# Second expert table: 64 of 256 tokens by gathered rows and VectorE passes, the other 192 in five TensorE passes for six

## The chip, the core and the metric

The kernel runs as one program on one core of one Trainium2 chip. The metric is the device time of one execution in microseconds (us), the median of several runs. The engines named below are TensorE (PE, its weight loads PEld), VectorE (DVE), ScalarE (ACT), GpSimd (POOL) and SyncE (SP), which here only issues DMAs.

## What is computed

One block on 256 tokens of width 2048: RMSNorm, an input projection, a state-space group and a windowed attention group, an output projection, and then the part that the change is about, a product-key retrieval of experts:

```python
def peer_ffn(xn, wq, keys, u_tab, v_tab):        # 16384 experts, 8 heads, top 16 of each
    q = (xf @ wq).reshape(t, PEER_HEADS, 2, PEER_HALF)
    sc = jnp.einsum("thpk,hpnk->thpn", q, keys)
    ...                                           # top 16 of both halves, top 16 of their sums
    gate = jax.nn.softmax(top, axis=-1)           # eidx, gate: 128 experts for each token
    u = jnp.take(u_tab, ib, axis=0)
    act = jax.nn.gelu(jnp.einsum("thkd,td->thk", u, xb), approximate=False)
    v = jnp.take(v_tab, ib, axis=0)
    return jnp.einsum("thk,thkd->td", gb * act, v)
...
h = h + peer_ffn(rmsnorm(h, norm2_g[i]), peer_wq[i], peer_keys[i], peer_u[i], peer_v[i])
return rmsnorm(h, norm_f_g)
```

All in float32. Each token uses 128 (head, expert) pairs of 16384 experts.

## The kernel before

Both expert tables are streamed whole, in 128 chunks of 128 experts (1 MB each), in two pieces of 512 KB. A ring of four pieces (`raw`, `high`, `low`) carries every streamed matrix of the kernel, and one chain serves it. SP loads a piece into `raw` (L325) when VectorE has finished the piece four before it in the ring (`lo_done`); ScalarE rounds it into `high` (L442), once TensorE has finished the piece four before it (`used`); VectorE forms the rest, `raw` minus `high`, in `low` (L686); TensorE multiplies. To reach float32 accuracy each product is three passes: high by high, high by low, low by high.

- **First table** (`product`, L1253 to L1255): for each chunk 48 matmuls of 256 columns give scores of 128 experts by 256 tokens; ScalarE takes them through Gelu into `big` (`expert_step`, L452). Meanwhile VectorE does the routing between its cuts (`route`, `center`, `share`), and GpSimd scatters the gates of the picked experts by 256 indirect DMAs with add (L430) into `gate_scratch`, a dense array of 128 chunks by 128 experts by 256 tokens in HBM, which SP cleared earlier.
- **Second table**: for each chunk VectorE multiplies Gelu and gates (`weights`, L1195), ScalarE rounds that (`round_w`, L653), VectorE forms the low part (L1198), and TensorE adds weights by table rows into all eight PSUM banks: 2 halves x 2 token blocks x 3 passes x 2 banks, 24 matmuls of 512 columns (`row_products`, L1476 to L1480). SP loads chunk after chunk, and behind the two pieces of each the gates of a chunk (`gate_load`, L377) after a wait on `w_ok`. VectorE's order in a chunk is: cut, gates, cut, low part of the weights.
- **End**: TensorE adds the residual from `h_back` (L1506); then for each block of 128 tokens follow square (L670), root (L674), VectorE's product (L1221) and the store (L409).

Of the kernel before, what the change touches and what calls it, by code (L numbers as in the profile page):

```python
# [20 lines left out]
ds = bass.ds  # L21
# [15 lines left out]

# [20 lines left out]
RING = 4  # L58

# [37 lines left out]
def build(nc, x_t, small, id_iota, w_in, w_out, w_q, keys, u_tab, v_tab, g_f, out):  # L97
    h_scratch = nc.dram_tensor("h_scratch", (P, KT * T), F32).ap()
    cs_scratch = nc.dram_tensor("cs_scratch", (1, SSD_HEADS * BLK), F32).ap()
    gate_scratch = nc.dram_tensor("gate_scratch", (N_KEYS, P, T), F32).ap()  # L100
    gate_cells = gate_scratch.rearrange("r c (t o) -> (r c t) o", o=1)

    with ExitStack() as ctx:
# [30 lines left out]
        w_lo = sb(ctx, "w_lo", 2 * T, F32R)
# [45 lines left out]
        SCORES = QZ  # L180
# [17 lines left out]
        assert ROUTE >= (ROUTE_CHUNKS + 8) * T and PICKS + 768 <= SCORES  # L198
# [3 lines left out]
        h_sum = view(XBC + 10 * T, T)  # L202
        rstd1 = view(TOK_T + 4 * SSD_HEADS, T)
# [82 lines left out]
        scattered = [sem(f"scattered{r}") for r in range(ROUTE_STEPS)]  # L286
        gate_back = [sem(f"gate_back{k}") for k in range(2)]
# [30 lines left out]
        def _(sp):  # L318
# [44 lines left out]
            def clear(group):  # L363

                dst = gate_scratch[ds(ZERO_CHUNKS * group, ZERO_CHUNKS)].rearrange("r c t -> c r t")
                src = zeros.rearrange("p (o t) -> p o t", o=1).broadcast_to([P, ZERO_CHUNKS, T])
                sp.dma_start(dst, src).then_inc(cleared, 16)
# [5 lines left out]
            sp.dma_start(h_scratch, h_sb).then_inc(h_saved, 16)  # L373
            load_all(u_tab, C_U, N_KEYS)
# [4 lines left out]
            for j in range(2):  # L379
                load(C_V_TAB + j, (C_V_TAB + j) % 2, v_tab[j])  # L380
            for r in range(ROUTE_STEPS):
                sp.wait_ge(scattered[r], 16 * TOPK)
# [13 lines left out]
            for q in range(H_PARTS + 2):  # L396
                second_table(q, q + 1)
                if q < H_PARTS:
                    n = KT * T // H_PARTS
# [5 lines left out]
            for tb in range(TB):  # L405
                for q in range(2):
                    sp.wait_ge(last_ok, 2 * tb + q + 1)
                    n = D // 2
                    sp.dma_start(out[tb * P:(tb + 1) * P, q * n:(q + 1) * n],  # L409
                                 big[:, (2 * tb + q) * n:(2 * tb + q + 1) * n]).then_inc(stored, 16)  # L410
            sp.wait_ge(stored, 16 * 2 * TB)
# [3 lines left out]
        def _(pool):  # L415
# [8 lines left out]
            for r in range(ROUTE_STEPS):  # L424
                h, tb = r // TB, r % TB
                pool.wait_ge(picks_ok, r // BATCH_STEPS + 1)
                if h:
                    pool.wait_ge(scattered[(h - 1) * TB + tb], 16 * TOPK)
                for at in range(r * TOPK, (r + 1) * TOPK):
                    nc.gpsimd.indirect_dma_start(  # L430
                        out=gate_cells, out_offset=bass.IndirectOffsetOnAxis(ap=cells_sb[:, at:at + 1], axis=0),
                        in_=gates_sb[:, at:at + 1], in_offset=None, compute_op=ALU.add).then_inc(scattered[r], 16)
# [3 lines left out]
        def _(act):  # L436
# [178 lines left out]
            with act.Fori(0, KT // 2 - 1) as i:  # L615
# [7 lines left out]
            def expert_step(c, par):  # L623
                cut_high(c + 1, 1 - par)
                at = (c - C_U) * T
                take(c, par, big[:, ds(at, T)], ACT.Gelu)

            def expert_pairs(lo, hi):
                with act.Fori(lo // 2, hi // 2) as i:
                    for j in range(2):  # L630
                        expert_step(C_U + 2 * i + j, (C_U + j) % 2)
# [6 lines left out]
            expert_pairs(0, 2)  # L638
            act.wait_ge(h_saved, 16)
            done = 2  # L640
            for b in range(ROUTE_BATCHES):
                expert_pairs(done, BATCH_CHUNKS * (b + 1) + 2)
                done = BATCH_CHUNKS * (b + 1) + 2
                soften(b)
            expert_pairs(done, ROUTE_CHUNKS + 8)
            act.wait_ge(picks_ok, ROUTE_BATCHES)
            expert_pairs(ROUTE_CHUNKS + 8, N_KEYS - 2)

            def round_w(e, par):
# [3 lines left out]
                nc.scalar.activation(w_hi[:, par * T:(par + 1) * T], w_full[par], ACT.Copy).then_inc(wh_ok, 1)  # L653

            expert_step(C_V_TAB - 2, C_V_TAB % 2)
            expert_step(C_V_TAB - 1, (C_V_TAB + 1) % 2)
            round_w(0, C_V_TAB % 2)
            with act.Fori(0, N_KEYS // 2 - 1) as i:
                for j in range(2):
                    e = 1 + 2 * i + j  # L660
                    par = (C_V_TAB + 1 + j) % 2
                    cut_high(C_V_TAB + e, par)
                    round_w(e, par)
            cut_high(C_END - 1, (C_END - 1) % 2)
            round_w(N_KEYS - 1, (C_END - 1) % 2)

            for tb in range(TB):
                act.wait_ge(sum_ok, tb + 1)
                acc = ps[:, 4 * tb:4 * tb + 4, :]
# [919 lines left out]
```

## Time and profile before

| what | value |
|---|---|
| median of 3 runs | 1900.62 us (1900.42 to 1902.73) |
| the profiled execution: its time / its span | 1903.04 us / 1901.2 us |
| granted TensorE clock, mean | 0.994 |
| busy share of the span: PE, DVE, ACT, POOL | 98%, 61%, 47%, 23% |
| second table, PE | about 1189 to 1892 us |

A row of the views has the engine's line, what it writes and reads, its count, the busy time and the mean of one, and then the time the engine sat idle before it and who ended that. The idle time of an engine that does not set the pace costs nothing. A busy TensorE is not one at its peak, since the ends of pipelined matmuls are modelled; the distance from start to start of equal steps is what a step costs.

### The profile page before, as it was taken

How to read it: one execution, taken by the hardware profiler on the slowest of the kernel's cores; microseconds unless marked ns; L12 is line 12 of the kernel's file. 1: busy time of each engine (PE TensorE's matmuls, PEld its weight loads, DVE VectorE, ACT ScalarE, POOL GpSimd, SP SyncE). 2: the span in 40 equal slices, each digit the busy share in tenths (PEclk: the TensorE clock that was granted, in tenths of full speed). 3: DMA queues.
4: the chain of work that ended last, by engine and by line, in shares of the span. 5: the costliest groups of instructions: out<-in, count | busy, mean ns of one | idle time of the engine just before them, and what ended most of it. 6: DMA issues, size and time to landing. Idle time of an engine off the chain costs nothing.

```text
span 1901.2 us, 36770 instructions
## 1 busy us (share of the span) xinstructions
PE 1861.1 (98%) x12735; PEld 1727.7 (91%) x12735; DVE 1153.9 (61%) x2075; ACT 899.3 (47%) x1212; POOL 431.4 (23%) x262
## 2 busy tenths in 40 slices
PE   7999979999999999999999999999999999999998
PEld 7998879999999999999999999888888888888886
DVE  7786676667888885344434434555555555555554
ACT  6545734434366666443344334444444444444443
POOL 0000000000028787877777710000000000000000
PEclk9999989999999999999999999999999999999999
DMA  7643548886557777777777765876666666666663
GB/s 246 216 174 134 166 134 271 276 254 225 181 176 183 183 183 177 191 183 178 184 185 183 177 184 175 279 240 217 217 217 219 217 213 220 215 218 216 220 215 117
DMA packets 167158, 383.03 MB, mean 201 GB/s; under 512 B 50240, under 2 KB 83152, under 8 KB 166736
## 3 DMA queue, kind: packets, MB, share of 16 engines
q1 hardware_dynamic: 130080, 379.25, 60.3%
q0 software_dynamic: 37040, 3.32, 5.7%
q8 instruction: 19, 0.31, 0.1%
q14 instruction: 19, 0.16, 0.0%
HBM read 361.37 MB, written 21.13 MB: 201 GB/s over the span
## 4 chain that ended last, share of the span: by engine, by line
PE 93%; DVE 2%; issue 2%; ACT 2%; DVEq 0%; DMA 0%; ACTq 0%; SPq 0%
PE ps L1253 18%; PE ps L1254 18%; PE ps L1255 18%; PE ps L1476 12%; PE ps L1480 12%; PE ps L1478 12%; ACT high L442 1%; PE ps L1506 0%; PE ps L1447 0%; DVE big L1012 0%; DVE big L1003 0%; DVE big L696 0%; DVE big L1014 0%; DVE big L984 0%; PE ps L1350 0%
## 5 line engine op out<-in xcount | busy, mean ns | idle before, releaser
L686 DVE TENSOR_TENSOR low<-raw,high 128x1024 fp32r<-128x1024 f32 x638 | 770.3, 1224 | 633.4 <-ACT high L442 586.0
L1253 PE MATMUL ps<-act_hi,high 128*128 128x256 f32 x3056 | 872.9, 286 | 24.3 <-DVE act_lo L719 13.1
L1254 PE MATMUL ps<-act_lo,high 128*128 128x256 f32 x3056 | 867.7, 284 | 0.0
L1255 PE MATMUL ps<-act_hi,low 128*128 128x256 f32 x3056 | 867.6, 284 | 0.0
L442 ACT ACTIVATE high<-raw 128x1024 fp32r<-128x1024 f32 x638 | 657.0, 1054 | 432.6 <-PE ps L1480 378.8
L1253 PEld LDWEIGHTS ps<-act_hi,high 128*128 128x128 f32 x3056 | 589.6, 193 | 29.0 <-issue 16.5
L1254 PEld LDWEIGHTS ps<-act_lo,high 128*128 128x128 f32 x3056 | 589.7, 193 | 0.1
L1255 PEld LDWEIGHTS ps<-act_hi,low 128*128 128x128 f32 x3056 | 589.6, 193 | 0.0
L430 POOL DMA_INDIRECT gate_scratch<-gates_sb,cells_sb x256 | 429.9, 1679 | 591.9 <-DVE gates_sb L1167 470.5
L1476 PE MATMUL ps<-high,w_hi 128*128 128x512 f32 x1024 | 315.5, 389 | 1.3 <-ACT big L452 1.3
L1480 PE MATMUL ps<-high,w_lo 128*128 128x512 f32 x1024 | 315.2, 389 | 0.0
L1478 PE MATMUL ps<-low,w_hi 128*128 128x512 f32 x1024 | 315.2, 389 | 0.0
L1476 PEld LDWEIGHTS ps<-high,w_hi 128*128 128x128 f32 x1024 | 192.0, 188 | 41.2 <-ACT big L452 1.5
L1480 PEld LDWEIGHTS ps<-high,w_lo 128*128 128x128 f32 x1024 | 192.2, 188 | 39.9
L1478 PEld LDWEIGHTS ps<-low,w_hi 128*128 128x128 f32 x1024 | 192.2, 188 | 39.9
L452 ACT ACTIVATE big<-ps 128x256 f32 (+1 forms) x128 | 49.3, 385 | 338.1 <-PE ps L1255 335.4
L591 ACT ACTIVATE act_hi<-big (+1 forms) x32 | 13.4, 418 | 95.0 <-DVE big L1014 52.6
L1198 DVE TENSOR_TENSOR w_lo<-side,w_hi 128x256 fp32r<-128x256 f32 x128 | 53.4, 418 | 2.4 <-ACT w_hi L653 2.4
L1195 DVE TENSOR_TENSOR side<-big,side 128x256 f32<-128x256 f32 x128 | 53.4, 418 | 0.0
L653 ACT ACTIVATE w_hi<-side 128x256 fp32r<-128x256 f32 x128 | 51.1, 399 | 0.8 <-DVE side L1195 0.8
L735 DVE TENSOR_TENSOR big<-ps,big 128x256 f32<-128x256 f32 (+2 forms) x47 | 19.7, 421 | 45.9 <-PE ps L1255 45.8
L452 ACT ACT_TABLE_LOAD x22 | 28.2, 1283 | 35.0 <-PE ps L1255 31.3
(158 smaller groups left out, 571.0 us busy)
## 6 DMA issues: line engine op xcount, KB each, us to landing
raw<-u_tab SPq DMA_DIRECT2D x256, 512.0 KB
raw<-v_tab SPq DMA_DIRECT2D x256, 512.0 KB
raw<-w_in SPq DMA_DIRECT2D x62, 512.0 KB
raw<-w_out SPq DMA_DIRECT2D x32, 512.0 KB
gate_scratch<-side SPq DMA_DIRECT2D x32, 512.0 KB, 6.8
raw<-w_q SPq DMA_DIRECT2D x32, 512.0 KB
side<-gate_scratch SPq DMA_DIRECT2D x128, 128.0 KB, 3.4
gate_scratch<-gates_sb,cells_sb POOLq DMA_INDIRECT x256
```

The source lines that it names most:

```text
L430: nc.gpsimd.indirect_dma_start(out=gate_cells, out_offset=bass.IndirectOffsetOnAxis(ap=cells_sb[:, at:at + 1], axis=0), in_=gates_sb[:, at ...
L442: nc.scalar.activation(slot(high, s), slot(raw, s), ACT.Copy).then_inc(hi_done, 1)
L452: nc.scalar.activation(dst, ps[:, par, 0:T], func).then_inc(taken, 1)
L686: V.tensor_tensor(slot(low, s), slot(raw, s), slot(high, s).bitcast(F32), ALU.subtract).then_inc(lo_done, 1)
L1195: V.tensor_tensor(w_full[par], gelu, gate_in[par], ALU.mult).then_inc(w_ok, 1)
L1198: V.tensor_tensor(w_lo[:, par * T:(par + 1) * T], w_full[par], w_hi[:, par * T:(par + 1) * T].bitcast(F32), ALU.subtract).then_inc(wl_ok, 1)
L1253: mm(acc, wh, a_hi, start=(kk == 0), stop=False)
L1254: mm(acc, wh, a_lo, start=False, stop=False)
L1255: ins = mm(acc, wl, a_hi, start=False, stop=(kk == KT - 1))
L1476: mm(acc[n], wh, vh[n], start=start, stop=False, skip_group_check=True)
L1478: mm(acc[n], wh, vl[n], start=False, stop=False, skip_group_check=True)
L1480: ins = mm(acc[n], wl, vh[n], start=False, stop=stop, skip_group_check=True)
```

## The change

Tokens 192 to 255 leave the second table's matmuls (`SPARSE` = 64, `DENSE` = 192). The first table is unchanged on TensorE, but ScalarE takes its result in two steps, 192 columns to `big` and 64 to `act_out`, and SP writes the latter to `act_scratch` in HBM, once every four chunks (32 DMAs). Gates are scattered densely for 192 tokens only: GpSimd issues 192 scatters and 8 small copies where it issued 256 scatters. The 64 x 128 picks of the other tokens are laid over 128 partitions, 64 in each (64 "units"). For each unit GpSimd gathers 128 rows of `v_tab`, of 8 KB each (1 MB), into one of three buffers; VectorE adds them, times gate times Gelu, to `acc_s` (128 x 2048). The Gelu values come by 64 gathers of one number for each partition. Before that, `acc_s` gets the residual of the 64 tokens by 16 transposes on TensorE and a copy on ScalarE, in the query stage. The unit stands behind the weights of a chunk, in 64 of the chunks 10 to 120. In the last chunks the two halves of `acc_s` are added and normalized.

For the dense 192 tokens the weights lie as [high of 64 tokens, high of 128, high of the 64 again, low of 64, low of 128]. One pass with 128 weight columns does high and low of the 64 tokens at once, a second their high by the table's low; the 128 tokens keep three passes. The part that came from the low weights lies in the partitions 64 to 127 of four banks, and is added at the end by four more matmuls.

```diff
+SPARSE = 64
+DENSE = T - SPARSE
+SLOTS_HALF = 8
+UNITS = SLOTS_HALF * PEER_HEADS
+ROWS = 3
+EXPORT = 4
+FIRST_UNIT, LAST_UNIT = 9, 121
...
@@ SP
-            load_all(u_tab, C_U, N_KEYS)
+            def save_act(g):
+                dst = act_scratch[EXPORT * g:EXPORT * (g + 1)].rearrange("r c t -> c r t")
+                sp.wait_ge(taken, C_U + EXPORT * (g + 1))
+                sp.dma_start(dst, act_out[g % 2].rearrange("p (r t) -> p r t", t=SPARSE)).then_inc(act_saved, 16)
...
             sp.wait_ge(used, 2 * C_V_TAB)
+            save_act(N_KEYS // EXPORT - 1)
@@ GpSimd, behind the scatters
+            def gather_row(n):
+                h, k = n // SLOTS_HALF, SLOTS_HALF + n % SLOTS_HALF
+                if n >= ROWS:
+                    pool.wait_ge(row_used, n - ROWS + 1)
+                nc.gpsimd.indirect_dma_start(
+                    out=row_in[n % ROWS], out_offset=None, in_=v_rows,
+                    in_offset=bass.IndirectOffsetOnAxis(ap=half_ix[:, h, 0, k:k + 1], axis=0)).then_inc(rows_in[n % ROWS], 16)
...
+            pool.wait_ge(act_saved, 16 * (N_KEYS // EXPORT))
+            for n in range(per):
+                gather_cell(n)
+            for n in range(UNITS):
+                for m in range(per + 4 * n, min(per + 4 * n + 4, UNITS)):
+                    gather_cell(m)
+                if n + ROWS < UNITS:
+                    gather_row(n + ROWS)
@@ ScalarE
-                take(c, par, big[:, ds(at, T)], ACT.Gelu)
+                nc.scalar.activation(view(e * DENSE, DENSE), ps[:, par, 0:DENSE], ACT.Gelu)
...
+                nc.scalar.activation(act_out[e // EXPORT % 2][:, at:at + SPARSE], ps[:, par, DENSE:T],
+                                     ACT.Gelu).then_inc(taken, 1)
...
-                nc.scalar.activation(w_hi[:, par * T:(par + 1) * T], w_full[par], ACT.Copy).then_inc(wh_ok, 1)
+                nc.scalar.activation(w_t[par][:, W_HI], w_full[:, :], ACT.Copy)
+                nc.scalar.activation(w_t[par][:, W_HI2], w_full[:, B_TOK], ACT.Copy).then_inc(wh_ok, 1)
@@ VectorE
+            def sparse_unit(n):
...
+                if n:
+                    dve.wait_ge(row_used, n)
+                else:
+                    dve.wait_ge(h_tok_ok, 1)
+                dve.wait_ge(rows_in[n % ROWS], 16 * (n // ROWS + 1))
+                V.scalar_tensor_tensor(out=acc_s, in0=row_in[n % ROWS], scalar=share_sb[:, n:n + 1], in1=acc_s,
+                                       op0=ALU.mult, op1=ALU.add).then_inc(row_used, 1)
...
+                cut_low_piece(C_V_TAB + e, par, 0)
+                weights(e, par, lambda: cut_low_piece(C_V_TAB + e, par, 1))
+                if unit < UNITS and (e - FIRST_UNIT + 1) * UNITS >= (unit + 1) * span:
+                    sparse_unit(unit)
+                    unit += 1
@@ TensorE
+            def narrow_rows(par, hf, start=False, stop=False):
...
+                for n in range(2):
+                    mm(acc[n], w[:, DENSE:DENSE + 2 * SPARSE], vh[n], start=start, stop=False, skip_group_check=True)
+                for n in range(2):
+                    ins = mm(acc[n][0:SPARSE], w[:, B_TOK], vl[n], start=False, stop=stop, skip_group_check=True)
...
-                    for tb in range(TB):
-                        ins = row_products(par, hf, tb, start=start)
-                    ins.then_inc(used, 1)
+                    narrow_rows(par, hf, start=start)
+                    wide_rows(par, hf, start=start).then_inc(used, 1)
...
+            pe.wait_ge(low_out, 1)
+            for n in range(4):
+                ins = mm(ps[0:SPARSE, 4 + n, :], ident[SPARSE:, SPARSE:], low_sb[SPARSE:, n * 512:(n + 1) * 512],
+                         start=False, stop=True, skip_group_check=True)
```

TensorE, the loop over the second table before: one half of a chunk (`high`, `low` are the table's parts, `w_hi`, `w_lo` the weights'; x2 is two banks).

```order
L1476 MATMUL ps<-high,w_hi 128x512 x2
L1478 MATMUL ps<-low,w_hi 128x512 x2
L1480 MATMUL ps<-high,w_lo 128x512 x2
L1476 MATMUL ps<-high,w_hi 128x512 x2
L1478 MATMUL ps<-low,w_hi 128x512 x2
L1480 MATMUL ps<-high,w_lo 128x512 x2
```

The same half of a chunk in the changed kernel (`w_even` holds all parts of the weights of an even chunk).

```order
L1665 MATMUL ps<-high,w_even 128x512 x2
L1667 MATMUL ps<-low,w_even 64x512 x2
L1677 MATMUL ps<-high,w_even 128x512 x2
L1679 MATMUL ps<-low,w_even 128x512 x2
L1681 MATMUL ps<-high,w_even 128x512 x2
```

Twelve matmuls are ten, and nothing else stands between them.

VectorE, the last chunk of the second table before (the loop's body has the same four operations):

```order
L686 TENSOR_TENSOR low<-raw,high 128x1024
L1195 TENSOR_TENSOR side<-big,side 128x256
L686 TENSOR_TENSOR low<-raw,high 128x1024
L1198 TENSOR_TENSOR w_lo<-side,w_hi 128x256
L1216 TENSOR_SCALAR big<-big 128x1
```

VectorE in the middle of the second table of the changed kernel, two chunks that follow each other, with a unit behind each:

```order
L821 TENSOR_TENSOR low<-raw,high 128x1024
L1366 TENSOR_TENSOR w_full<-big,side 128x192
L821 TENSOR_TENSOR low<-raw,high 128x1024
L1369 TENSOR_TENSOR w_odd<-w_full,w_odd 128x192
L1357 SCALAR_TENSOR_TENSOR big<-big,share_sb 128x2048
L821 TENSOR_TENSOR low<-raw,high 128x1024
L1366 TENSOR_TENSOR w_full<-big,side 128x192
L821 TENSOR_TENSOR low<-raw,high 128x1024
L1369 TENSOR_TENSOR w_even<-w_full,w_even 128x192
L1357 SCALAR_TENSOR_TENSOR big<-big,share_sb 128x2048
```

A unit (`L1357`) now stands between a chunk's weights and the next chunk's first cut, in 4 of 7 chunks, and the two operations on weights are a quarter narrower.

## Rows read from the trace of the kernel before

**Rows 1.** The page: busy us of each engine (share of the span); the chain's shares.

```profile
PE 1861.1 (98%) x12735; PEld 1727.7 (91%) x12735; DVE 1153.9 (61%) x2075; ACT 899.3 (47%) x1212; POOL 431.4 (23%) x262
...
PE 93%; DVE 2%; issue 2%; ACT 2%; DVEq 0%; DMA 0%; ACTq 0%; SPq 0%
```

**Rows 2.** Busy us (instructions) of each engine, PEclk, DMA share, GB/s by stretches.

```profile
1110.00:1180.00 70.00, 70.00 (x586) 70.00 (x585) 29.04 (x25) 27.91 (x36) 0.00 (x0) 1.00 0.54 181
1300.00:1400.00 100.00, 100.00 (x443) 82.79 (x442) 57.09 (x75) 44.77 (x55) 0.00 (x0) 1.00 0.65 215
600.00:700.00 100.00, 99.95 (x831) 99.55 (x830) 88.67 (x305) 66.21 (x74) 77.38 (x46) 1.00 0.73 182
```

**Rows 3.** Groups by line, second table, 1300 to 1800 us.

```profile
L686 DVE TENSOR_TENSOR low<-raw,high 128x1024 fp32r<-128x1024 f32 x185 | 226.8, 1226 | 214.5 <-ACT high L442 214.5
L1476 PE MATMUL ps<-high,w_hi 128*128 128x512 f32 x736 | 226.5, 389 | 0.0
...
L442 ACT ACTIVATE high<-raw 128x1024 fp32r<-128x1024 f32 x184 | 195.2, 1061 | 277.1 <-PE ps L1480 277.1
...
L1198 DVE TENSOR_TENSOR w_lo<-side,w_hi 128x256 fp32r<-128x256 f32 x92 | 38.4, 418 | 0.0
...
L653 ACT ACTIVATE w_hi<-side 128x256 fp32r<-128x256 f32 x92 | 36.7, 399 | 0.0
```

**Rows 4.** VectorE in order of time, second table: start, us, operation, idle before it.

```profile
1190.16 0.42 DVE L1195 TENSOR_TENSOR side<-big,side 128x256 f32<-128x256 f32 x1
1190.50 1.22 DVE L686 TENSOR_TENSOR low<-raw,high 128x1024 fp32r<-128x1024 f32 x1
...
1200.90 1.23 DVE L686 TENSOR_TENSOR low<-raw,high 128x1024 fp32r<-128x1024 f32 x1 [1.16 <-ACT high L442]
1202.04 0.42 DVE L1198 TENSOR_TENSOR w_lo<-side,w_hi 128x256 fp32r<-128x256 f32 x1
...
1207.48 0.42 DVE L1198 TENSOR_TENSOR w_lo<-side,w_hi 128x256 fp32r<-128x256 f32 x1
```

**Rows 5.** The DMA view, 1300 to 1800 us.

```profile
DMA packets 39699, 108.37 MB, mean 217 GB/s; under 512 B 4414, under 2 KB 16190, under 8 KB 39699
...
side<-gate_scratch SPq DMA_DIRECT2D x92, 128.0 KB, 3.2
```

**Rows 6.** The DMA view, 8 to 16 us, reads in rows of 4 KB.

```profile
DMA packets 1152, 3.27 MB, mean 409 GB/s; under 512 B 256, under 2 KB 384, under 8 KB 1152
...
q1 hardware_dynamic: 1152, 3.27, 103.2%
```

**Rows 7.** Stretches as in rows 2, around the start of the second table.

```profile
1188.00:1196.00 8.00, 7.40 (x33) 6.13 (x34) 5.56 (x8) 4.78 (x7) 0.00 (x0) 1.00 0.93 290
1189.00:1190.00 1.00, 1.00 (x6) 0.82 (x5) 0.98 (x1) 0.94 (x1) 0.00 (x0) 1.00 0.98 213
```

**Rows 8.** DMA issues: KB each, median us to landing.

```profile
h_back<-h_scratch SPq DMA_DIRECT2D x4, 512.0 KB, 6.5
...
g_last<-g_f SPq DMA_DIRECT2D x2, 512.0 KB, 5.5
```

**Rows 9.** Groups by line, whole span, the nearest kin of what is added.

```profile
L1263 PE MATMUL ps<-big,side 128*128 128x256 f32 x42 | 11.3, 430 | 2.5 <-ACT big L556 2.5
...
L1506 PE MATMUL ps<-consts,h_back 128*128 128x128 f32 x64 | 7.5, 275 | 0.0
...
L984 DVE SCALAR_TENSOR_TENSOR big<-big,side 128x256 f32<-128x256 f32 x16 | 6.7, 478 | 0.1
...
L1221 DVE SCALAR_TENSOR_TENSOR big<-ps,big,g_last 128x1024 f32<-128x1024 f32 x4 | 5.0, 1280 | 0.1
```

**Rows 10.** The chain in order of time, its end: start, us, what.

```profile
1879.77 3.57 PE ps L1506 x32
...
1892.41 1.98 ACT big L670 x2
1895.62 1.28 DVE big L1221
```

More of the change, by code:

```diff
@@ L202, in build @@
         h_sum = view(XBC + 10 * T, T)
+        GELUS = N_KEYS * DENSE
+        row_in = [view(GELUS + k * D, D) for k in range(ROWS)]
+        low_sb = view(GELUS, D)
+        acc_s = view(GELUS + ROWS * D, D)
+        assert GELUS + ROWS * D >= SCORES + TB * 2 * PEER_HEADS * N_KEYS and GELUS + (ROWS + 1) * D <= N_KEYS * T
         rstd1 = view(TOK_T + 4 * SSD_HEADS, T)
@@ L286, in build @@
         scattered = [sem(f"scattered{r}") for r in range(ROUTE_STEPS)]
+        swapped = sem("swapped")
+        act_saved = sem("act_saved")
+        cell_ok = sem("cell_ok")
+        cell_in = [sem(f"cell_in{b}") for b in range(ROUTE_BATCHES)]
+        rows_in = [sem(f"rows_in{k}") for k in range(ROWS)]
+        row_used = sem("row_used")
+        h_turned = sem("h_turned")
+        h_tok_ok = sem("h_tok_ok")
+        half_moved = sem("half_moved")
+        s_summed = sem("s_summed")
+        s_squared = sem("s_squared")
+        s_var = sem("s_var")
+        s_root = sem("s_root")
+        s_done = sem("s_done")
+        s_stored = sem("s_stored")
+        low_sum = sem("low_sum")
+        low_out = sem("low_out")
         gate_back = [sem(f"gate_back{k}") for k in range(2)]
@@ new lines, in _ @@
+            for b in range(ROUTE_BATCHES):
+                pool.wait_ge(picks_ok, b + 1)
+                hs = slice(2 * b, 2 * b + 2)
+                nc.gpsimd.dma_start(half_v[0:SPARSE, hs, :, SLOTS_HALF:], swap_v[SPARSE:, hs, :, 0:SLOTS_HALF]).then_inc(swapped, 16)
+                nc.gpsimd.dma_start(half_v[SPARSE:, hs, :, 0:SLOTS_HALF], swap_v[0:SPARSE, hs, :, SLOTS_HALF:]).then_inc(swapped, 16)
+                scatter(2 * b, 0)
+                pool.wait_ge(swapped, 32 * (b + 1))
+                scatter(2 * b, 1)
+                scatter(2 * b + 1, 0)
+                scatter(2 * b + 1, 1)
@@ L435, in _ @@
+            nc.gpsimd.dma_start(row_in[1][0:SPARSE], acc_s[SPARSE:]).then_inc(half_moved, 16)
+            pool.wait_ge(s_done, 1)
+            nc.gpsimd.dma_start(out[DENSE:], acc_s[0:SPARSE]).then_inc(s_stored, 16)
         @block.scalar
@@ L1030, in _ @@
             inverse_root(3, rs_v[:, 0:T], rs_r[:, 0:T], [(7, T, 0, D)])
+            own.step(V.memset(acc_s[SPARSE:], 0.0))
             def score_take(m, j):
@@ L1166, in share @@
                 own.settle()
-                V.tensor_tensor(by_head(gates_sb[:, cols]), part, wide(r_total), ALU.mult).then_inc(picks_ok, 1)
+                part = by_block(pick[2])
+                per_head = r_total.rearrange("p (h b o) -> p b h o", b=TB, o=1)
+                own.step(V.tensor_tensor(first(gates_sb), part[:, 0], per_head[:, 0].broadcast_to([P, 2, TOPK]), ALU.mult))
+                for dst in (half_v, swap_v):
+                    ins = V.tensor_tensor(dst[:, hs, 1, :], part[:, 1], per_head[:, 1].broadcast_to([P, 2, TOPK]), ALU.mult)
+                ins.then_inc(picks_ok, 1)
             own.step(V.tensor_tensor(r_diag, ident, iota, ALU.mult))
@@ L1204, in v_step @@
+            unit = 0
+            half_s = slice(0, SPARSE)
+            for e in range(1, N_KEYS):
+                par = (C_V_TAB + e) % 2
                 cut_low_piece(C_V_TAB + e, par, 0)
                 weights(e, par, lambda: cut_low_piece(C_V_TAB + e, par, 1))
-            with dve.Fori(0, N_KEYS // 2 - 1) as i:
-                for j in range(2):
-                    v_step(1 + 2 * i + j, (C_V_TAB + 1 + j) % 2)
-            v_step(N_KEYS - 1, (C_END - 1) % 2)
-            dve.wait_ge(gf_in, 16 * 2)
```

294 lines of the change are left out of this document (197 added, 97 removed).

## Prediction

> **What bounds the kernel now.** Read the page first: TensorE is busy in 98% of the span and is 93% of the chain that ended last [rows 1]. Then the stretches, since each stage has its own limit: in both tables TensorE is busy 100% at the full granted clock (1.00, its level of 2.4 GHz), VectorE 41% and 57%, ScalarE 40% and 45% [rows 2]. Then the groups of the second table with their idle times: ScalarE's rounding sat idle 277.1 of 500 us, and what ended that was a matmul; VectorE's cut sat idle 214.5 us until the rounding [rows 3]. So ScalarE waits for TensorE, VectorE for ScalarE, and TensorE for nobody. A step costs its distance from start to start: the low part of the weights starts at 1202.04 and again at 1207.48, so a chunk takes 5.44 us, and each of its 24 matmuls 5.44/24 = 0.2267 us [rows 4] (389 ns, the mean in rows 3, is one matmul with its pipeline).
>
> The question is what comes next when TensorE needs less. Two resources get work for what TensorE gives up: VectorE, and the 16 DMA engines.
>
> **TensorE.** Four matmuls fewer in each of 128 chunks: 512 x 0.2267 = 116.1 us less. The passes with 64 weight columns still stream 512 columns, so they count in full. A chunk is then 20 x 0.2267 = 4.53 us.
> Added on TensorE: 16 transposes with float32 operands in the query stage. The nearest step is the residual's, 16 of which (32 instructions) take 3.57 us [rows 10]: +3.6 us, on the path, since TensorE has no idle time in the stages around it.
> Added at the end: the residual matmuls stay 32 in number, and four matmuls of 512 float32 columns fold the low part. One of 256 such columns is two instructions of about 0.22 us from start to start (11.3 us for 42 gives 0.27 as upper bound) [rows 9], so one of 512 columns is about 0.9 us: 3.6 us in front of the last sum. Behind that the end is the old one, 1892.4 to 1901.2 [rows 10]. The two blocks' squares and products still fit one behind the other: the wide block's sum is ready about 3.4 us ahead of the last one, VectorE's two products of one block take 2 x 1.28 us [rows 9]. So +3.6 us.
>
> **VectorE, by chunk.** From start to start a cut takes 1202.04 - 1200.90 = 1.14 us and an operation on 256 columns of weights 1190.50 - 1190.16 = 0.34 us [rows 4]; on 192 columns I take 0.28. A unit is one operation over 2048 columns, which no row shows. Between 256 columns at 478 ns and 1024 at 1280 ns a column costs 1.04 ns [rows 9], so 2048 take 1280 + 1024 x 1.04 = 2350 ns. With a unit in 4 of 7 chunks: 2 x 1.14 + 2 x 0.28 + 2.35 x 4/7 = 4.18 us against TensorE's 4.53: 92%, not the bound, but it was 54%.
> A unit may hold up the chain even so. Put TensorE's end of chunk e-2 at 0. ScalarE rounds the second piece of chunk e until 1.3 and the weights until 1.8, VectorE is through at about 2.7, and TensorE wants chunk e at 4.53. A unit from 2.7 to 5.0 delays the next chunk's first cut, whose rounding was done at 3.5; that chunk is through at 7.8, wanted at 9.06. If a second unit stands there, the third chunk is through at 12.9, wanted at 13.6, and then comes a chunk without one. The margin stays above 0.7 us, so I cost the units at nothing while the loads come in time. Without that margin each of 64 units costs 2 x 1.14 + 0.56 + 2.35 - 4.53 = 0.66 us, 42 us in all.
>
> **ScalarE** rounds two pieces (1061 ns each) and the weights in two steps, at most 2 x 399 ns [rows 3]: 2.9 of 4.53 us. In the first table it takes the scores in two steps, at most 0.4 us more of a chunk in which it is idle for over half [rows 2]. The split and the save to `act_scratch` lie ahead of the first weights and of the load of chunk 2 on SP: +1.0 us (0 to 4), for about 0.4 us stand on TensorE's path. **GpSimd** and the additional operations of `share` lie beside a TensorE that is 99.95% busy where VectorE is busy 88.67 of 100 us [rows 2]; 64 fewer scatters more than pay for the 8 copies. The 32 saves run in pieces of 256 B where the DMA share is 0.54 to 0.73 [rows 2]; the ring has 2 chunks, 11 us, to hide them: 0 (up to 5). The longer straight-line code I cost at nothing (0 to 3).
>
> **DMA, by chunk.** In steady state a chunk brings 1.049 MB of table and 0.131 MB of gates at 217 GB/s [rows 5], share 0.65 [rows 2]. New: 1.049 + 0.098 (gates of 192 tokens) + 4/7 x 1.049 (a unit's 128 rows of 8 KB) = 1.746 MB in 4.53 us, that is 385 GB/s. That is 1.8 times today's rate, and the dearest new resource. What can 16 engines do? Three readings bound it:
> - a full queue of 4 KB rows moved 409 GB/s for 8 us, with a third of the packets small [rows 6]: 1.746/0.409 = 4.27 us, under TensorE's 4.53;
> - today's share as if it were linear: 217/0.65 = 334 GB/s: 5.23 us;
> - the stretch at the start of the second table, where gates, `h_back` and table are asked for together: 290 GB/s at share 0.93 [rows 7], as linear 312 GB/s: 5.60 us.
> I build the value from packets. In rows 6, 8 us x 16 engines x 1.032 = 132 engine-us went to 768 packets of 4 KB and 384 small ones: 0.155 us for 4 KB. Rows of 1 KB move 213 GB/s at share 0.98 [rows 7], so about 0.075 us each. A chunk then needs (256 + 4/7 x 256) x 0.155 + 128 x 0.07 + about 1 for the completions = 72.4 engine-us, over 16 engines 4.53 us: just TensorE's own pace. Two streams whose requests wait on consumers will not keep every engine full; I take 95%, 4.77 us. Gathers run from chunk 10 to about 116, some 107 chunks: 107 x (4.77 - 4.53) = +25.7 us.
> A rule of the Trainium skill speaks against even that much. "DMA: Bandwidth & Descriptors", section Specifications, gives about 358 GB/s as the limit of HBM for a core. The 409 GB/s of rows 6 are above it for 8 us, so this trace does not agree. By it a chunk takes 4.88 us and the term is +37 us, not +26.
>
> **The sum**, against the profiled execution's own 1903.0 us: 1903.0 - 116.1 + 3.6 + 3.6 + 1.0 + 25.7 = 1820.8. The median of the runs is 2.4 us lower, 1900.6: so 1818.4, say 1819 us.
>
> **The rivals.**
> (a) TensorE sets the pace all through, DMA and units stay hidden: 1795.1 - 2.4 = 1793 us. For it: 409 GB/s, and three row buffers that hold 5 chunks' worth of gathers. Against it: it needs 385 GB/s over 500 us of two streams, which no row shows.
> (b) The DMA engines have one flat ceiling midway between the readings of 409 and 312 GB/s, 360: 1.746/0.360 = 4.85 us, 107 x 0.32 = +34: 1827 us, between 1822 and 1845 (340 GB/s). For it: of rows 2 and 7 no stretch shows over 290. Against it: rows 6. The limit of the skill's page named above, 358 GB/s, is this case with a cause of its own, and gives 1830.
> (c) The linear reading is right, 334 GB/s: 107 x (5.23 - 4.53) = +75: 1868 us. For it: rows 5 and 7 give 312 to 334 by themselves. Against: rows 6 shows packets overlapping at a share over 1, so a share below 1 overstates what a packet needs.
> (d) VectorE's units find no margin because each load is late: +42 us over (a), 1835 us.
> (e) Slower than before: the gathers crowd out SP's loads. A piece is loaded only after the cut of the piece four before it, so two chunks take at least one load's landing L, the rounding 1.06, the cut 1.14, some 0.7 for signals and 0.7 for a unit in the way: a chunk takes (L + 3.6)/2. Today a load of 128 KB behind a piece lands in 3.2 us [rows 5], pieces behind others in 5.5 to 6.5 us [rows 8]. At L = 5.5 the chunk is 4.55, still hidden; at L = 6.5 it is 5.05, +56 us. The saving of 107.9 us is used up when 107 chunks take 5.54 us each, at L = 7.5; at L = 8 a chunk takes 5.8 and the time is 1929 us. For it: up to 3 MB of gathers can stand in GpSimd's queue at once, beside 1 MB of SP's. Against it: VectorE needs a unit only every 7.9 us, so if engines share evenly a gather is in flight for 5.2 of 7.9 us, SP has 200 GB/s in that time and 400 in the rest, 268 on the mean against the 253 that it needs.
> The skill's page named above has in its section "Queues, rings and completion order" that an engine takes its queues in turn by packets; if a gather's packets are the larger ones, SP gets less than half. No row shows both queues under load.
> That the change does nothing can be left out: the matmuls are gone from TensorE's order.
>
> **How the numbers follow.** Forecast (chunks at 4.65 to 4.80 us, 1806 to 1822): 0.42. (a) 0.17, (b) 0.13, (c) 0.14, (d) 0.04, (e) 0.10. The likeliest gives 1819. The range leaves out (e) and the upper part of (c), to 1880, and reaches down to (a) less its small terms, 1792. A measurement can tell 0.2%, some 4 us. Faster: all but (e), 0.90; within 0.2%, a point inside (e), 0.01; slower 0.09.
>
> **What would show it.** TensorE's start-to-start of matmuls stays 0.227 us; chunks 0 to 9 and 117 to 127 take 4.53 us each. In the middle a chunk takes 4.77, and the chain of waits there runs TensorE from VectorE's cut, that from ScalarE, that from a load of `v_tab`. The DMA view shows about 366 GB/s and a share near 1.0. Under (a) ScalarE still waits for TensorE and the rate is 385; under (b) and (c) the rate is flat at 360 or 334 in every slice; under (d) VectorE has no idle time; under (e) the rate falls below 315 while raw pieces take over 7.5 us to land. The prediction is wrong if TensorE's stretch in the first table grows, or if VectorE waits on `rows_in`: I have three buffers hide each gather, 16 us ahead.

## The result and the profile after

The changed kernel takes 1835.9 us (median of 4 runs, 1833.4 to 1842.1) against 1901.4 of the kernel before: a ratio of 0.966, 95% interval 0.963 to 0.969. That is 65 us less; the forecast was 82 less, and the range held the time. The profiled execution took 1842.05 us, span 1840.3, and was the slowest of the four, so what is read from its trace lies some 6 us above the median.

The page of the changed kernel: busy times, the DMA share and GB/s by fortieths of the span, and the chain's shares.

```profile
PE 1771.6 (96%) x12247; PEld 1605.1 (87%) x12247; DVE 1282.2 (70%) x2166; ACT 874.5 (48%) x1434; POOL 521.6 (28%) x336
...
DMA  7554538776557778777777555599999999999994
GB/s 252 204 189 138 175 91 252 229 244 217 191 188 189 188 189 189 189 188 189 189 188 257 188 188 188 196 307 334 358 342 348 359 359 351 338 363 348 347 322 127
...
PE 67%; DMA 15%; DVE 8%; issue 5%; ACT 4%; SPq 0%; DVEq 0%; ACTq 0%
```

TensorE is still busy in 96% of the span, but its share of the chain fell from 93% [rows 1] to 67%, and DMA stands in it with 15%. From the 27th of the 40 slices to the last but one, the second table, the DMA share is 9 tenths and more.

Busy time of PE, PEld, DVE, ACT and POOL (with counts), granted clock, DMA share and GB/s, in the late first table and in the middle of the second:

```profile
1000.00:1100.00 100.00, 100.00 (x836) 100.00 (x835) 41.51 (x36) 39.77 (x68) 0.00 (x0) 1.00 0.59 186
1250.00:1750.00 500.00, 474.61 (x2000) 354.94 (x1999) 422.94 (x461) 259.61 (x402) 145.01 (x95) 0.99 0.95 350
```

The first table is as it was [rows 2]. In the second, TensorE is idle for 25 of 500 us, and the engines move 350 GB/s where they moved 215. VectorE is busy 85%, was 57%.

The groups of VectorE and ScalarE there, and the waits (engine, line, waited for: us, times, longest):

```profile
L821 DVE TENSOR_TENSOR low<-raw,high 128x1024 fp32r<-128x1024 f32 x200 | 244.3, 1222 | 54.4 <-ACT high L553 52.9
L553 ACT ACTIVATE high<-raw 128x1024 fp32r<-128x1024 f32 x202 | 214.0, 1060 | 182.0 <-DMA raw<-v_tab 144.2 <-PE ps L1681 36.1
L1357 DVE SCALAR_TENSOR_TENSOR big<-big,share_sb 128x2048 f32<-128x2048 f32 x58 | 136.0, 2346 | 0.1
...
L1366 DVE TENSOR_TENSOR w_full<-big,side 128x192 f32<-128x192 f32 x100 | 35.3, 353 | 23.8 <-DMA side<-gate_scratch 23.6
```

```profile
ACT high L553 <- DMA raw<-v_tab: 144.2, 118, 4.2
DVE low L821 <- ACT high L553: 52.9, 77, 3.3
PEld ps L1665 <- DVE low L821: 38.7, 31, 3.5
ACT high L553 <- PE ps L1681: 36.1, 40, 2.7
...
DVE w_full L1366 <- DMA side<-gate_scratch: 23.6, 17, 2.3
```

The reader is to compare this with [rows 3]. There ScalarE's rounding waited 277 us for TensorE. Here it waits 144 us for a load of `v_tab`, 118 times of 202, and 36 us for TensorE. The chain is turned round: ScalarE waits for DMA, VectorE for ScalarE, TensorE for VectorE.

The DMA view of the same stretch (KB each, median us to landing):

```profile
DMA packets 52757, 174.79 MB, mean 350 GB/s; under 512 B 7005, under 2 KB 19817, under 8 KB 45438
...
raw<-v_tab SPq DMA_DIRECT2D x200, 512.0 KB, 6.3
side<-gate_scratch SPq DMA_DIRECT2D x100, 96.0 KB, 6.4
big<-v_tab,half_sb POOLq DMA_INDIRECT x57, 9.1
```

A piece now lands 6.3 us after it was asked for, and the gates after 6.4 where the kernel before had 3.2 [rows 5]; for the pieces of the second table before no landing is on record. A unit's gather takes 9.1 us and is in time: VectorE has no wait for `rows_in`. The median for the pieces rests on 50 of the 200 loads, those whose landing the trace has, and they differ widely:

```profile
DMA to landing us min/median/max: 3.1/6.3/8.7
```

How long a chunk takes is read from TensorE, from the first matmul of a chunk (L1665) to the first of the next: 4.60 us where it waits for nobody, as in the chunks 118 to 125, without gathers; 4.99 us on the mean of the 107 chunks from 10 on (5.00 below). It is not an even pace. Of the 107 chunks 71 take under 4.75 us; 21 take more than 5.2, up to 7.8, and hold 34 of the 42 us that the 107 take beyond 4.60 each.

Three small terms. TensorE in order of time, in a stretch where it waits for nobody, two matmuls in each row:

```profile
1217.10 0.63 PE L1667 MATMUL ps<-low,w_even 128*64 128x512 f32 x2
...
1219.40 0.63 PE L1667 MATMUL ps<-low,w_even 128*64 128x512 f32 x2
```

From one half of a chunk to the next 2.30 us pass for ten matmuls, 0.230 us each; before it was 0.2267. The 16 transposes of the residual and the four last matmuls, by line:

```profile
L1718 PE MATMUL ps<-big,consts 64*64 64x512 f32 x8 | 3.6, 595 | 0.0
...
L1638 PE MATMUL ps<-consts,big 128*64 128x128 f32 x16 | 1.9, 272 | 0.0
```

And the end of the chain:

```profile
1815.61 3.64 PE ps L1705 x32
...
1827.67 1.98 ACT big L805 x2
```

The end lasts from 1815.6 to 1840.3, 24.7 us; before, 1879.8 to 1901.2 [rows 10], 21.4. The four matmuls of L1718 run behind the sum of the 128 tokens, from 1827.6 to 1831.2, and the square of the 64 tokens starts at 1831.24.

### The profile page after: what moved, and what is told of

It reads as the page before. It is cut to its first block, busy times and chain, and to the rows that moved or that the text cites. A ratio compares the mean times of both kernels' runs of the same rounds, so it can differ in the third digit from the quotient of the medians.

```text
span 1840.3 us, 34226 instructions
## 1 busy us (share of the span) xinstructions
PE 1771.6 (96%) x12247; PEld 1605.1 (87%) x12247; DVE 1282.2 (70%) x2166; ACT 874.5 (48%) x1434; POOL 521.6 (28%) x336
## 4 chain that ended last, share of the span: by engine, by line
PE 67%; DMA 15%; DVE 8%; issue 5%; ACT 4%; SPq 0%; DVEq 0%; ACTq 0%
PE ps L1435 19%; PE ps L1436 18%; PE ps L1437 18%; DMA raw<-v_tab 12%; DVE low L821 4%; DMA side<-gate_scratch 4%; ACT high L553 3%; PE ps L1665 2%; PE ps L1679 2%; PE ps L1681 2%; PE ps L1667 2%; PE ps L1677 2%; DVE big L1357 1%; DVE w_full L1366 0%; DVE big L831 0%
## 5 line engine op out<-in xcount | busy, mean ns | idle before, releaser
L497 POOL DMA_INDIRECT gate_scratch<-gates_sb,cells_sb x128 | 213.2, 1666 | 66.2 <-issue 66.2
L517 POOL DMA_INDIRECT big<-v_tab,half_sb x64 | 99.7, 1558 | 362.5 <-DVE big L1357 358.8
L525 POOL DMA_INDIRECT share_sb<-act_scratch,cell_ix x64 | 92.7, 1448 | 239.2 <-DMA act_scratch<-side 220.0
L1357 DVE SCALAR_TENSOR_TENSOR big<-big,share_sb 128x2048 f32<-128x2048 f32 x64 | 150.1, 2346 | 0.1
L497 POOL DMA_INDIRECT gate_scratch<-half_sb x64 | 108.1, 1689 | 19.5 <-issue 19.5
L1665 PE MATMUL ps<-high,w_even 128*128 128x512 f32 x256 | 81.7, 401 | 15.7 <-DVE w_even L1369 14.1
L1665 PE MATMUL ps<-high,w_odd 128*128 128x512 f32 x256 | 81.7, 401 | 12.4 <-DVE w_odd L1369 12.2
L1667 PE MATMUL ps<-low,w_odd 128*64 128x512 f32 x256 | 80.9, 397 | 0.0
L1679 PE MATMUL ps<-low,w_even 128*128 128x512 f32 x256 | 80.7, 396 | 0.0
L1681 PE MATMUL ps<-high,w_odd 128*128 128x512 f32 x256 | 80.5, 396 | 0.0
L1679 PE MATMUL ps<-low,w_odd 128*128 128x512 f32 x256 | 80.5, 396 | 0.0
```

Of the source, the lines that this page charges most:

```text
L497: nc.gpsimd.indirect_dma_start(out=gate_cells, out_offset=bass.IndirectOffsetOnAxis(ap=ix, axis=0), in_=v, in_offset=None, compute_op=ALU. ...
L517: nc.gpsimd.indirect_dma_start(out=row_in[n % ROWS], out_offset=None, in_=v_rows, in_offset=bass.IndirectOffsetOnAxis(ap=half_ix[:, h, 0, ...
L1357: V.scalar_tensor_tensor(out=acc_s, in0=row_in[n % ROWS], scalar=share_sb[:, n:n + 1], in1=acc_s, op0=ALU.mult, op1=ALU.add).then_inc(row_ ...
L1665: mm(acc[n], w[:, DENSE:DENSE + 2 * SPARSE], vh[n], start=start, stop=False, skip_group_check=True)
L1667: ins = mm(acc[n][0:SPARSE], w[:, B_TOK], vl[n], start=False, stop=stop, skip_group_check=True)
L1679: mm(acc[n], wh, vl[n], start=False, stop=False, skip_group_check=True)
```

## The experiments

The question was what holds a chunk at 5.00 us where TensorE needs 4.60. Three answers: the DMA engines are full (ceiling); VectorE has no margin with the units; or the ring is too short for the time that a load now takes (loop). The time is that of one run, or the median of several where a ratio is given. e1 to e5 leave out or spoil a part of the result: their times show what a piece of work costs. The mean of a chunk is read as above, from chunk 10 to chunk 117. In rows of stretches the columns are those of [rows 2].

### e1: units without gathers

```diff
 def gather_row(n):
+    if n < ROWS:                      # only the first three
         nc.gpsimd.indirect_dma_start(...)
...
-    dve.wait_ge(rows_in[n % ROWS], 16 * (n // ROWS + 1))
+    dve.wait_ge(rows_in[n % ROWS], 16)
```

> The gathers of rows are left out after the first three; VectorE's 64 units of 2048 columns stay and use old rows, so the 64 tokens' sums are not computed. Measured so far: a chunk takes 5.00 us in the middle of the second table, and TensorE's own pace there is 4.60. Theory DMA (the 16 DMA engines are full): chunks go to 4.60 us everywhere, time 1836 - 43 = 1793 us. Theory VectorE (the units leave no margin): chunks stay near 5.0, time 1830 to 1836.

1800.1 us. The middle of the second table:

```profile
1250.00:1750.00 500.00, 500.00 (x2176) 384.94 (x2175) 454.02 (x499) 278.39 (x436) 55.39 (x39) 1.00 0.76 250
```

TensorE is without a gap and a chunk takes 4.60 us, with VectorE busy 454 of 500 us. So the units alone hold nothing back where loads come in time; the loss comes with the gathers. From the low part of the first chunk's weights to that of the last it is 624.8 - 582.6 = 42 us between the two profiled executions, and 36 us between this run and the changed kernel's median.

### e2: gathers of half the bytes

```diff
-    out=row_in[n % ROWS], out_offset=None, in_=v_rows,
+    out=row_in[n % ROWS][:, 0:PIECE], out_offset=None, in_=v_halves,   # rows of 4 KB
```

> Each gather after the first three brings rows of 4 KB instead of 8 KB, as many of them; the units stay whole, so half of each sum uses old data. Theory DMA by bytes (350 GB/s): 1.446 MB / 0.350 = 4.13 us, below TensorE's pace, so 4.60 us and 1793 us. Theory DMA by requests (a row costs the same whatever its size): 5.0 and 1836. Theory VectorE: 1836.

1806.7 us, chunks of 4.66:

```profile
1250.00:1750.00 500.00, 497.09 (x2147) 378.55 (x2146) 451.54 (x495) 277.43 (x429) 157.43 (x98) 1.00 0.90 309
```

Near TensorE's pace. The bytes of a row count, the number of requests does not hold the kernel at 5.00; but at 309 GB/s and a share of 0.90 a small loss is left already, which a ceiling of 350 doesn't explain.

### e3: all gathers, units of 64 columns

```diff
-    V.scalar_tensor_tensor(out=acc_s, in0=row_in[n % ROWS], ..., in1=acc_s, ...)
+    V.scalar_tensor_tensor(out=acc_s[:, 0:64], in0=row_in[n % ROWS][:, 0:64], ..., in1=acc_s[:, 0:64], ...)
```

> All gathers stay; a unit on VectorE works on 64 columns instead of 2048, so most of the 64 tokens' sums are left out. Theory DMA: a chunk stays at 4.95 to 5.0 us at 350 GB/s, time 1828 to 1836. Theory VectorE: 4.60 and 1793.

1830.3 us, chunks of 4.85:

```profile
1250.00:1750.00 500.00, 482.15 (x2061) 364.78 (x2060) 317.78 (x474) 266.40 (x413) 115.81 (x97) 0.99 0.98 360
```

VectorE is busy 318 instead of 423 of 500 us, and the time is 6 us less, which one run against a spread of 9 us hardly shows. VectorE as the bound is ruled out, also with loads that come late. But the same bytes went at 360 GB/s, not at 350. That is a first sign against a fixed ceiling, though a weak one: the profiled execution of the changed kernel was its slowest.

### e4: plain copies in place of gathers

```diff
-    nc.gpsimd.indirect_dma_start(out=row_in[n % ROWS], ..., in_=v_rows, in_offset=...)
+    nc.gpsimd.dma_start(row_in[n % ROWS], v_tab[(37 * n) % N_KEYS])
```

> In place of a gather of picked rows GpSimd copies one whole chunk of the table, the same 1 MB in the same 128 rows of 8 KB but contiguous and not indirect; the sums use wrong rows. Theory DMA by bytes: no change, 1830 to 1840. Theory that scattered rows or indirect descriptors are the cost: chunks of 4.6 to 4.8 us, 1793 to 1815.

1827.0 us, chunks of 4.86, 360 GB/s in 1250 to 1750 us. 9 us less than the median, 6 less than the fastest run of the changed kernel. That the rows are scattered and the descriptors indirect costs at most some 9 of the 36 us; how much of the 9 is the spread, one run does not say.

### e5: no loads of gates

```diff
-    sp.wait_ge(w_ok, 2 * i + j + 1)
-    gate_load(2 * i + j + 2, par)
```

> The gates of chunks 2 to 127 are not loaded (old gates are used, so the sums are wrong); all else stays. It takes 128 rows of 768 B from each chunk: 5.6% of the bytes but a quarter of the packets. Theory that the DMA engines are limited by bytes (350 GB/s): 1.648/0.350 = 4.71 us for a chunk, time 1836 - 31 = 1805 us. Theory that each packet has a price (0.07 us or more for a small one): 76.8 - 9 = 67.8 engine-us, 4.4 us, so TensorE's pace of 4.60, 1795 us. Theory that the load's landing behind the gathers sets the pace whatever the share: 4.9 and 1828.

1829.4 us, chunks of 4.87:

```profile
1250.00:1750.00 500.00, 483.38 (x2052) 362.44 (x2051) 429.58 (x472) 261.44 (x410) 150.83 (x97) 0.99 0.93 338
```

The first two forecasts fail: with 26% of the packets gone (39235 of 52757 are left in 500 us) the time should have fallen by 30 us or more by either reading of a full engine. It fell by 6, and the DMA share fell to 0.93. Engines that are the bound don't get idle when work is taken from them. The third forecast fits, 4.9 us and 1828: the landing of a load sets the pace, whatever the share. The edit also takes out SP's wait for `w_ok`, but in the changed kernel SP waited for VectorE's cuts alone (304.5 us of 500).

### e6: the 64-column pass with 128 weight columns

```diff
-    ins = mm(acc[n][0:SPARSE], w[:, B_TOK], vl[n], ...)
+    ins = mm(acc[n], w[:, 0:P], vl[n], ...)
```

> The pass over the table's low part for the 64 tokens gets 128 weight columns instead of 64 (what it adds in the partitions 64 to 127 is wrong). A pair of matmuls is 0.460 us from start to start in the changed kernel and was 0.4533. If the switch between 64 and 128 weight columns costs that: 0.4533 again, about 6 us off the light chunks and little in the full ones, 1830 to 1835. If not, no change: 1834 to 1840.

1836.8 us, but TensorE's rows, two matmuls each, read:

```profile
1214.67 0.62 PE L1667 MATMUL ps<-low,w_odd 128*128 128x512 f32 x2
...
1216.93 0.62 PE L1667 MATMUL ps<-low,w_odd 128*128 128x512 f32 x2
```

2.26 us for ten matmuls, 2.30 before. The 64-column pass among 128-column passes costs 0.03 to 0.04 us in each half of a chunk. In chunks that wait for loads it is not seen.

### e7: the gates of four chunks in one load

```diff
-    gate_scratch = nc.dram_tensor("gate_scratch", (N_KEYS, P, DENSE), F32).ap()
+    gate_scratch = nc.dram_tensor("gate_scratch", (N_KEYS // 4, P, 4 * DENSE), F32).ap()
+    v_quads = v_tab.rearrange("(m a) c d -> m (a c) d", a=4).rearrange("m (c s) d -> m c s d", s=4)
...
+    for e in range(2, N_KEYS):        # written out
+        load(C_V_TAB + e, (C_V_TAB + e) % 2, v_quads[e // 4, :, e % 4, :])
+        if e % 4 == 2 and e // 4 + 1 < N_KEYS // 4:
+            sp.wait_ge(w_ok, e - 1)
+            gate_load(e // 4 + 1)     # 128 rows of 3 KB
```

> Chunks are laid out as expert = 512 m + 4 c + s, so that the gates of four chunks lie side by side for each partition, and come in one load of rows of 3 KB, one group ahead; the stores of the Gelu values and the clearing of the gates get rows four times as long as well. All 256 tokens are computed as in the reference. Same bytes, 96 packets fewer of 446 in a chunk. Theory packets: 128 x 0.07 turn into 32 x about 0.13 engine-us, 5 engine-us or 0.3 us less of a chunk: 4.7 us, 1836 - 32 = 1804 us. Theory bytes: 5.0 and 1830 to 1836, less the 24 us in which VectorE waits for gates at most.

1823.2 us (6 runs, 1814.5 to 1825.3), ratio 0.9595 (0.958 to 0.961). The gain is 13 us, where the count of packets gave 32, and bytes 0 to 6 and up to 24 more for the waits for gates: that doesn't decide between them. The run changed three things at once, the layout, the loading in fours and SP's loop, which e9 and e12 take apart in part.

### e8: a ring of six pieces

```diff
+    raw_more = sb(ctx, "raw_more", 2 * PIECE)      # where act_hi, act_lo were
...
+    for half in range(2):
+        n = 2 * e + half
+        if n >= 6:
+            sp.wait_ge(lo_done, 2 * C_V_TAB + n - 5)   # six pieces back, not four
+        sp.dma_start(raw_slot(n), ...)
```

> The changed kernel with six pieces of raw for the second table instead of four (the two new ones lie where the first table's activations were); bytes, packets, gathers and units are the same, and a load may be asked for two pieces earlier. Theory ceiling (the 16 DMA engines are full at 350 GB/s): 1830 to 1836, chunks of 4.95 to 5.0 us. Theory loop (a piece is asked for only after the cut four pieces before it, and lands 6.3 us later beside the gathers: (6.3 + 3.6)/2 = 4.95 us for a chunk): with six pieces (6.3 + 3.6)/3 = 3.3 us, no limit; then chunks of 4.6 to 4.75 us as far as the engines can (at most about 375 GB/s), 1800 to 1812.

1799.8 us (4 runs, 1799.5 to 1802.0), ratio 0.947 (0.945 to 0.949). Stretch, landing times, waits:

```profile
1250.00:1750.00 500.00, 500.00 (x2176) 385.36 (x2175) 455.12 (x500) 278.82 (x435) 170.66 (x98) 1.00 1.00 376
```

```profile
raw<-v_tab SPq DMA_DIRECT2D x144, 512.0 KB, 7.7
raw_more<-v_tab SPq DMA_DIRECT2D x73, 512.0 KB, 7.8
```

```profile
ACT high L560 <- PE ps L1693: 165.3, 153, 1.5
...
ACT high L560 <- DMA raw<-v_tab: 3.9, 2, 2.0
...
ACT high L560 <- DMA raw_more<-v_tab: 1.2, 2, 0.6
```

All gathers, all units, the same bytes, and TensorE has no gap: chunks of 4.60 us, and the time of e1, where all but three gathers of rows were left out. The engines move 376 GB/s. A piece lands later than before, after 7.7 us instead of 6.3, and hardly anybody waits for it: 5.1 us in all, where it was 144. So 350 GB/s was not a ceiling. It was, but for the loops that e12 takes out of the account, the result of how early the ring let SP ask.

### e9: the layout of e7, gates one chunk at a time

```diff
+    v_chunk = lambda e: v_quads[e // 4, :, e % 4, :]
-    sp.dma_start(gate_in[par], gate_scratch[e])
+    sp.dma_start(gate_in[par], gate_scratch[e // 4, :, g:g + DENSE])   # 128 rows of 768 B as before
```

> The layout of e7 (expert = 512 m + 4 c + s, table rows of a piece 32 KB apart instead of 8, longer rows in the first table's stores), but the gates of each chunk come by themselves, in 128 rows of 768 B one chunk ahead, as in the changed kernel. If the loading of gates in fours was what brought e7 its 12 us: 1832 to 1838. If it was the layout: 1820 to 1826.

1818.3 us (4 runs, 1811.6 to 1822.6), ratio 0.956 (0.953 to 0.959). No slower than e7, so the loading in fours brought nothing; what is left is the layout and SP's written-out loop. Chunks take 4.74 us here and 4.73 in e7.

### e12: the control, loops written out

```diff
-    with sp.Fori(first, end) as i:
-        for j in range(2):
-            load(C_V_TAB + 2 + 2 * i + j, par, v_tab[2 * i + j + 2])
+    for e in range(2, N_KEYS):
+        load(C_V_TAB + e, (C_V_TAB + e) % 2, v_tab[e])
...
-    with act.Fori(0, N_KEYS // 2 - 3) as i:
+    for e in range(1, N_KEYS - 5):
```

> The changed kernel with the second table's loops on SP and ScalarE written out, as e8 to e11 have them (e7 and e9 on SP alone), and with the ring of four pieces and the plain layout: the control for those runs. If the written-out loops were part of their gain, e.g. because SP asks for a piece sooner: 1815 to 1828. If the two more pieces (e8) and the layout (e7, e9) did it: 1832 to 1840, chunks of 4.95 to 5.0 us at 350 GB/s.

1829.2 us (4 runs, 1824.0 to 1830.8), ratio 0.961 (0.959 to 0.962):

```profile
1250.00:1750.00 500.00, 483.54 (x2059) 361.16 (x2058) 432.66 (x473) 263.52 (x409) 148.29 (x99) 1.00 0.98 361
```

Just above the first forecast, below the second: of the 36 us that e8 gains, some 7 are the written-out loops and 29 the two pieces (10 and 26 by the ratios). The layout may be worth another 11 us with a ring of four (e9 against e12); the intervals of the two ratios touch, and e9 wrote out SP's loop alone, this run ScalarE's too, so that is not settled. With six pieces it is worth nothing, as e10 shows.

### e10 and e11: all together

e10 is e7 and e8 together; e11 adds to it 128 weight columns in every pass:

```diff
+    W_ZERO, W_HI, W_HI2, W_LO = slice(0, 64), slice(64, 256), slice(256, 320), slice(320, 512)
...
-    ins = mm(acc[n][0:SPARSE], w[:, B_TOK], vl[n], ...)
+    ins = mm(acc[n], w[:, 0:P], vl[n], ...)       # 64 zeros, then the high part
```

> e7 and e8 together. Theory loop: the ring no longer holds back, the engines' capacity does, chunks of 4.60 to 4.65 us, 1795 to 1803. Theory ceiling: as e7, 1820 to 1825.

1801.0 us (one run): as e8, and chunks of 4.60. The forecast was right for the pace, and the layout adds nothing to it.

> e10, and 64 columns of zeros in front of the weights, so that the pass over the table's low part for the 64 tokens has 128 weight columns like the others, with the reference's result (its sum goes to the partitions 64 to 127 and is folded at the end). A chunk at TensorE's pace is then 4.53 us instead of 4.60: 5 to 8 us less than e10, if the DMA engines can follow (385 GB/s); otherwise the same as e10.

1791.9 us (4 runs, 1791.4 to 1793.4), ratio 0.9425 (0.941 to 0.944), 44 us less than the changed kernel:

```profile
1250.00:1750.00 500.00, 500.00 (x2208) 414.12 (x2207) 460.87 (x507) 283.34 (x443) 172.82 (x99) 1.00 0.99 379
```

Chunks of 4.53 us with every gather in place, at 379 GB/s. It is the fastest kernel of this study.

## Why the prediction came out as it did

**The range and the direction were right, the size of one term was not.** Against the profiled execution the sum was 1820.8, and the execution took 1842.05. Term by term:

- TensorE, 512 matmuls fewer: forecast -116.1. The pace in the new mixture is 0.230 us, not 0.2267, a chunk 4.60 and not 4.533, so it is -116.1 + 128 x 0.066 = -107.6 in chunks without a wait. The step that the 64-column passes "count in full" was too kind: e6 shows that they cost slightly more than in full.
- Transposes: forecast +3.6, measured 1.9 us for 16. The row taken for it counts 32 instructions for 16 tiles, a transpose here is one. The low part of the first chunk's weights comes at 1188.5 instead of 1188.07, so all that lies before the second table, for which +3.6 and +1.0 were forecast, came to +0.4.
- The end: forecast +3.6, measured 24.7 - 21.4 = +3.3. Right, and for the reason given: the four matmuls stand before the last sum.
- **DMA: forecast +25.7, measured +42.** This is the term that was mis-sized. Sum: 1903.0 - 107.6 + 0.4 + 3.3 + 42 = 1841.

So the forecast was 21 us too low: 16 by DMA and 8 by TensorE, less 4 by what lies ahead of the second table, which by luck hid a part of the miss.

**Which step of the DMA term failed.** The term asked how many engine-us a chunk needs and to what share two streams fill the engines, 72.4 engine-us at 95%. The share came out as taken, 0.95, and yet a chunk took 5.00 us, not 4.77: 0.95 x 16 x 5.00 is 76 engine-us. In e8 the same packets took at most 4.60 x 16 = 73.6, in e12 0.98 x 16 x 4.86 = 76.2. The busy time of the engines is no fixed price of packets, and their capacity did not set the pace: in e8 they follow at 4.60 us, and in e11, where the gates come in fewer packets, at 4.53. What the term left out is the way round the ring, which stood under rival (e): a chunk takes (L + 3.6)/2. I used this formula only for the case that ends slower than before, and not for the forecast, where L = 5.5 was taken as hidden without asking what L would be. With the measured median of 6.3 us it gives 4.95 us, and measured are 5.00. That this is so near is in part luck: with the medians of e6, e7, e9 and e12 (6.6, 6.2, 6.3 and 6.7) it gives 0.2 to 0.3 us more than their chunks take, and with the landings from 3.1 to 8.7 us of the changed kernel's own trace anything from 3.4 to 6.2. A load that lands late stops the chain, and one that lands early gives nothing back, since TensorE goes no faster than 4.60. Why L rises from about 3 us to 6.3 no run takes apart; my reading is that evenly shared engines, as worked out under (e), leave SP 268 GB/s for the 253 that it needs, and so near to its share a queue forms.

**The rivals.** (a), TensorE sets the pace, is what six pieces of ring make of it (e8, e11), not this kernel. (b), one flat ceiling of 340 to 360 GB/s, has the measured 1836 in its band of 1822 to 1845, and is wrong as a cause: 376 and 379 GB/s went through in e8 and e11. The Trainium skill's "DMA: Bandwidth & Descriptors", section Specifications, has about 358 GB/s as the limit of HBM for a core, got there as half of what a stack gives to two cores. Over 500 us these runs, with one core at work, moved 376 and 379, so the measurement decides against it as a limit here. (c) is refuted by the same rows. (d) had the nearest number of all, 1835 us, and is wrong too. e1 alone doesn't decide it, since there the loads come in time. e3 does: with all gathers and units of 64 columns the chunks still take 4.85, and beside late loads the units cost about 6 us of the median, not 42. (d)'s own sign fails as well, since VectorE was idle for 77 of 500 us. (e) is the mechanism, at a small size: L was 6.3, and it had to pass 7.5 to end slower.

In order of time one case can be followed in the changed kernel. VectorE, GpSimd, SP, ScalarE, TensorE:

```profile
1400.44 2.35 DVE L1357 SCALAR_TENSOR_TENSOR big<-big,share_sb 128x2048 f32<-128x2048 f32 x1
1402.70 1.22 DVE L821 TENSOR_TENSOR low<-raw,high 128x1024 fp32r<-128x1024 f32 x1
```

```profile
1403.53 1.20 POOL L517 DMA_INDIRECT big<-v_tab,half_sb  x1 [4.47 <-DVE big L1357]
```

```profile
1404.10 1.72 SPq L373 DMA_DIRECT2D raw<-v_tab  x2
```

```profile
1412.84 1.06 ACT L553 ACTIVATE high<-raw 128x1024 fp32r<-128x1024 f32 x1 [4.19 <-DMA raw<-v_tab]
```

```profile
1416.97 0.72 PE L1665 MATMUL ps<-high,w_even 128*128 128x512 f32 x2 [1.75 <-DVE w_even L1369]
```

The unit at 1400.44 pushes the next cut to 1402.70. When that cut is done SP asks for the piece four further on, at 1404.10, just behind GpSimd's request for a unit's 1 MB at 1403.53. ScalarE can round this piece only at 1412.84, 8.7 us after it was asked for; it had been idle 4.19 us by then, and TensorE idles 1.75 us before the chunk. Later cut, later request, later landing, later cut: the loop closes over four pieces, so a delay is handed on to the chunk two further on. It does not go on for ever: TensorE's late chunks come mostly singly or in pairs (7.00 and 6.30, 7.78 and 6.05), with chunks of 4.60 behind them.

**What was foreseen and held**: a unit takes 2346 ns (forecast 2350), an operation on 192 columns 0.27 us from start to start (0.28); the gathers are in time with three buffers; VectorE's margin is enough where loads come in time (e1); the first table doesn't change; in the middle the chain runs TensorE from VectorE's cut, that from ScalarE, that from a load of `v_tab`; the bytes (1.746 MB in a chunk: 350 GB/s x 5.00 us).

**What stays open.** Why the written-out loops bring 7 us, and whether the layout brings 11 with a short ring. Why a load takes 3.1 us one time and 8.7 another: a gather in flight is the natural suspect, and no run moved the gathers against the loads. The 3.6 is a sum of estimates, and a median of L tells little about a pace that single late loads make. So the formula names the mechanism, and its size only to about 5%.

## What to carry to other kernels

When a change puts a second stream beside a streamed ring, work out the loop before the bandwidth: landing time under the new load plus the steps up to the slot's release, divided by the chunks that the ring holds, is an estimate of the pace it can keep, and the slow landings count more than the median. A DMA share of 0.95 to 0.98 does not say that the engines are the bound: give the loads a longer lead (two more pieces here, in memory that was already free) and see whether the rate goes up. Two more pieces on the path of requests were worth 29 us here; fewer packets, plain instead of indirect copies and a shorter VectorE operation were each worth under 10.

## What the runs showed of the hardware

- 16 DMA engines moved 376 to 379 GB/s for 500 us from two queues at once, loads in rows of 4 KB and gathers in rows of 8 KB (e8, e11); the share in these rows was 0.99 to 1.00, while 361 GB/s already read 0.98 (e12), and 0.95 went with 350 (the changed kernel). The share is near 1 well before the rate is at its best.
- With both queues loaded, a load of 512 KB lands after 6.3 us (median of the 50 that the trace has, 3.1 to 8.7) and a gather of 1 MB after 9.1; in the first table of the same kernel the median is 3.2 us.
- Scattered rows of 8 KB by indirect gathers went nearly as fast as plain copies of the same size (some 9 us of 1836 apart, one run, e4).
- One pass with 64 weight columns between passes with 128 costs 0.03 to 0.04 us more in each half of a chunk, though the streamed columns are the same (e6: 2.26 against 2.30 us for ten matmuls).
